# Up projection of a feed-forward layer as seven block products in place of eight, with weight sums made by accumulating DMA

## What is computed

```python
h = rmsnorm(x, norm_ffn_pre)
u = h @ w_up                              # (512, 1024) @ (1024, 5632): 2816 gate, 2816 value columns
u = conv_b + sum(conv_w[j] * shift(u, 2 - j) for j in range(3))   # causal, along the tokens
f = gelu(u[:, :2816]) * u[:, 2816:]
x = x + rmsnorm(f @ w_down, norm_ffn_post)
```

## Time and profile before

| | us |
|---|---|
| median of 3 runs | 632.87 (632.45 to 634.44) |
| profiled execution: device time | 632.87 |
| its span, first to last instruction | 631.1 |
| up projection, sweep 0 (in half units) | about 277 to 302 |
| up projection, sweeps 1 to 10 | 302 to 520 |
| down projection | 520 to 625 |

### The profile page before, as it was taken

The page is one execution under the profiler, slowest core; times in us unless marked ns, Lnnn a source line. Parts: engine busy times, 40 slices in busy tenths (PEclk is TensorE's granted clock), DMA queues, the critical chain, the costliest instruction groups (busy, mean ns, idle before and its releaser), DMA issues.

```text
span 631.1 us, 8616 instructions
## 1 busy us (share of the span) xinstructions
PE 618.7 (98%) x3048; PEld 510.3 (81%) x3048; DVE 418.0 (66%) x619; ACT 313.6 (50%) x505; POOL 102.1 (16%) x112
## 2 busy tenths in 40 slices
PE   7999999999999999999999999999999999999996
PEld 6888778778787877899888888888888888887885
DVE  3457548657755875984755556556565668988786
ACT  5457338526735834663533334343333336656661
POOL 5413103111210402421000000000000013532203
PEclk9999999999999999999999999999999999999999
DMA  9744223331513254642423233333323436999933
GB/s 273 205 124 136 76 68 100 101 95 41 159 38 98 103 206 160 196 138 69 133 86 104 79 98 100 100 100 93 107 84 103 162 69 112 180 226 230 230 88 133
DMA packets 91947, 78.90 MB, mean 125 GB/s; under 512 B 2617, under 2 KB 76521, under 8 KB 91922
## 3 DMA queue, kind: packets, MB, share of 16 engines
q1 hardware_dynamic: 84434, 61.79, 32.0%
q0 software_dynamic: 7488, 16.80, 13.3%
HBM read 76.46 MB, written 2.12 MB: 125 GB/s over the span
## 4 chain that ended last, share of the span: by engine, by line
PE 81%; DVE 7%; DMA 4%; POOL 3%; ACT 2%; issue 2%; DVEq 0%; SPq 0%; POOLq 0%; ACTq 0%
PE bank L539 73%; DVE ws L1490 2%; DMA raw<-in_w_down_dram 2%; PE bank L681 1%; PE bank L619 1%; DMA raw<-in_w_in_dram 1%; POOL grstd L473 1%; DMA late<-in_w_down_dram 1%; PE bank L670 1%; DVE xs L1306 1%; PE bank L610 1%; PE bank L609 1%; DVE hT L1466 1%; PE bank L550 1%; POOL work L477 1%
## 5 line engine op out<-in xcount | busy, mean ns | idle before, releaser
L539 PE MATMUL bank<-hT,ws 128*128 128x512 f32 (+1 forms) x1872 | 410.2, 375 | 1.6 <-DVE work L1284 0.6
L539 PEld LDWEIGHTS bank<-hT,ws 128*128 128x128 f32 x1872 | 328.7, 188 | 63.2 <-issue 2.5
L539 PE MATMUL bank<-ws,yT 128*128 128x512 f32 x468 | 110.0, 391 | 0.2 <-DVE late L1510 0.2
L1189 DVE TENSOR_TENSOR ws<-raw,ws 128x1024 fp32r<-128x1024 f32 x85 | 103.5, 1218 | 6.9 <-ACT ws L875 6.4
L539 PEld LDWEIGHTS bank<-ws,yT 128*128 128x128 f32 x468 | 87.0, 188 | 18.5 <-DVE late L1510 0.6
L875 ACT ACTIVATE ws<-raw 128x1024 fp32r<-128x1024 f32 x88 | 92.6, 1053 | 15.5 <-PE bank L539 11.5
L1096 ACT ACTIVATE gains<-bank,conv 128x512 f32<-128x512 f32 x22 | 17.2, 781 | 76.8 <-PE bank L539 76.8
L1450 DVE SCALAR_TENSOR_TENSOR gains<-bank,conv,gains 128x511 f32<-128x511 f32 x22 | 16.5, 749 | 53.8 <-ACT gains L1096 53.8
L522 POOL DMA_DIRECT2D late<-in_w_down_dram x8 | 10.7, 1335 | 253.2 <-DVE ws L1490 253.2
L1096 ACT ACTIVATE rot<-bank,conv 128x512 f32<-128x512 f32 x22 | 17.2, 780 | 63.8 <-PE bank L539 63.8
L539 PE MATMUL bank<-ws,hT 128*128 128x512 f32 x186 | 42.8, 389 | 0.0
(11 more groups left out here) (135 smaller groups left out, 605.9 us busy)
## 6 DMA issues: line engine op xcount, KB each, us to landing
raw<-in_w_up_dram SPq DMA_DIRECT2D x44, 512.0 KB, 3.8
raw<-in_w_in_dram SPq DMA_DIRECT2D x28, 512.0 KB, 4.3
raw<-in_w_out_dram SPq DMA_DIRECT2D x16, 512.0 KB, 3.3
raw<-in_w_down_dram POOLq DMA_DIRECT2D x12, 512.0 KB, 7.7
raw<-in_w_down_dram SPq DMA_DIRECT2D x9, 512.0 KB, 4.2
late<-in_w_down_dram POOLq DMA_DIRECT2D x8, 512.0 KB, 5.8
xs<-in_x_dram SPq DMA_DIRECT2D x6, 512.0 KB, 4.1
late<-in_w_down_dram SPq DMA_DIRECT2D x6, 512.0 KB, 7.3
```

The lines of the kernel that those rows point to most:

```text
L539: return nc.tensor.matmul(dst, st, mv, start=start, stop=stop, skip_group_check=onto)
L1189: nc.vector.tensor_tensor(ws[:, c, 1, :], raw[:, c, :], f32(ws[:, c, 0, :]), ALU.subtract).then_inc(w_lo, 1)
```

## The change

Sweeps 0 and 1 stay as they are (`PLAIN = 2`); sweep 1 uses the other four banks. From sweep 2 on, a sweep is a 2x2x2 block product. The blocks of its output are gate and value columns (256 each) by left and right half of the tokens (256 each); the contraction is halved (4 tiles of 128 rows). Seven products take the place of eight: each is one unit of 2 column tiles x 4 row tiles x 3 matmuls = 24 matmuls, of 256 columns. Four sums of h blocks (`tF`) are made by DVE and split once, at the start; hF keeps a copy of h for this (`h_keep`). The weight sums are accumulating DMAs from POOL (`up_add`). The products run in the order 7, 1, 4, 3 of the sweep before, 6, 2, 5. Their results are joined in part in PSUM (products 6, 5, 3 and 4 accumulate onto what is there, "onto") and in part by ACT copies (`kept7`, `s1`, `kept4`) and DVE sums (`vneg` left and right, `c11`). The value half comes out negated, and its taps are stored negated. The taps, gelu and product of a sweep run beside the next sweep. Weight splits run three units ahead in place of two. `F_EARLY`, the f differences and the start of the down projection are reordered. The diff, cut:

```diff
+PLAIN = 2
+UP_UNITS = [("plain", i, j) for i in range(PLAIN) for j in range(4)]
+for _i in range(PLAIN, SWEEP - 1):
+    UP_UNITS += [(7, _i), (1, _i), (4, _i)] + [(3, _i - 1)] * (_i > PLAIN) + [(6, _i), (2, _i), (5, _i)]
+UP_UNITS += [(7, SWEEP - 1), (1, SWEEP - 1), (4, SWEEP - 1), (6, SWEEP - 1), (3, SWEEP - 2), (5, SWEEP - 1),
+             (2, SWEEP - 1), (3, SWEEP - 1)]
+UP_LOADS = {7: (0, 0), 1: (0, 0), 4: (1, 1), 2: (0, 1)}
+UP_ADDS = {7: (1, 0), 6: (1, 1), 3: (0, 1), 5: (1, 0)}
+DOWN0 = UP0 + len(UP_UNITS)
...
-F_EARLY = {(2, 1): (0,), (4, 1): (1,), (6, 1): (2,), (6, 3): (3,), (8, 1): (4,), (8, 3): (5,), (9, 1): (6,), (10, 1): (7,)}
-F_SLOTS = 16
-F_AHEAD = 6
+F_EARLY = {(4, 7): (0,), (4, 8): (1,), (4, 9): (2,), (4, 10): (3,), (6, 10): (4,), (5, 10): (5,), (2, 10): (6,)}
+F_DIFF = {(4, 3): 0, (4, 5): 1, (1, 8): 2, (1, 10): 3}
+F_SLOTS = 17
+F_AHEAD = 5
...
+    return {7: i % 2, 6: i % 2, 3: i % 2, 4: 2 + i % 2, 5: 2 + i % 2, 1: 4, 2: 5}[p]
...
+        hF = part(5120, 2048).rearrange("p (k c) -> p k c", k=KT)
+        tF = [part(7168 + 1024 * m, 1024).rearrange("p (k c) -> p k c", k=4) for m in range(4)]
+        T_OF = {7: 0, 4: 1, 6: 2, 5: 3}
...
+        UP_BANK = [(0, 1, 5, 6), (2, 3, 4, 7)]
+        X_BANK, Y_BANK = [(0, 1), (2, 3)], [(5, 6), (4, 7)]
...
+            for i in range(PLAIN, SWEEP):
+                for p in (4, 1, 7, 2):
+                    n = UP0 + UP_AT[p, i]
+                    if raw_slot_of(n) < 4 or i > PLAIN:
+                        sp.wait_ge(w_lo, lo_count(before_in_slot(n)))
+                    sp.dma_start(up_raw(n).rearrange("p (k n) -> p k n", k=4), up_block(UP_LOADS[p], i)
...
+            def up_add(p, i):
+                n = UP0 + UP_AT[p, i]
+                c = raw_slot_of(n)
+                if p == 7:
+                    pool.wait_ge(raw_loaded[c], 16 * loads_of_slot(n))
+                else:
+                    pool.wait_ge(w_lo, lo_count(before_in_slot(n)))
+                pool.dma_start(up_raw(n).rearrange("p (k n) -> p k n", k=4), up_block(UP_ADDS[p], i),
+                               accum_op=ALU.add).then_inc(raw_added[c], 16)
+            up_add(7, PLAIN)
+            for i in range(PLAIN, SWEEP):
+                up_add(6, i)
+                up_add(5, i)
+                if i + 1 < SWEEP:
+                    up_add(7, i + 1)
+                up_add(3, i)
...
+            def up_product(n):
+                p, i = UP_UNITS[n]
+                c, done = slot_of(UP0 + n), i - PLAIN
+                pe.wait_ge(w_lo, lo_count(UP0 + n))
+                if p in T_OF:
+                    pe.wait_ge(t_lo, T_OF[p] + 1)
+                if p == 7:
+                    if done < 2:
+                        pe.wait_ge(gtap0, 2 * (i - 1))
+                        pe.wait_ge(vtap0, 2 * (i - 1))
+                    else:
+                        pe.wait_ge(c11_done, done - 1)
+                if p == 1:
+                    pe.wait_ge(gtap0, 2 * (i - 1))
+                    if done < 2:
+                        pe.wait_ge(vtap0, 2 * (i - 1))
+                if p == 4:
+                    pe.wait_ge(p7_kept, done + 1)
+                if p == 6:
+                    pe.wait_ge(p1_kept, done + 1)
+                if p == 2:
+                    pe.wait_ge(p4_kept, done + 1)
+                if p == 5:
+                    pe.wait_ge(v_left, done + 1)
+                if p == 3:
+                    pe.wait_ge(v_right, done + 1)
+                onto = p in (6, 5, 3, 4)
+                lo = 0 if p in (7, 4) else 256
+                for r in range(2):
+                    b = (X_BANK if p in (1, 6, 5, 3) else Y_BANK)[i % 2][r]
+                    for k in range(4):
+                        cols = slice(k * 256 + r * P, k * 256 + r * P + P)
+                        for m in range(3):
+                            ins = three(bank[b][:, lo:lo + 256], ws[:, c, 0, cols], ws[:, c, 1, cols],
+                                        t_block(p, 0)[:, k, :], t_block(p, 1)[:, k, :], m,
+                                        not onto and k == 0 and m == 0, k == 3 and m == 2, onto)
+                ins.then_inc(unit_done, 1)
...
+            def up_post(n):
+                act.wait_ge(unit_done, UP0 + n + 1)
+                if n < 4 * PLAIN:
+                    _, i, j = UP_UNITS[n]
+                    if j % 2 == 0:
+                        gate_tap2(i, j // 2, bank[UP_BANK[i][j]][:])
+                    else:
+                        value_tap2(i, j // 2, bank[UP_BANK[i][j]][:])
+                        gate_gelu(i, j // 2)
+                    return
+                p, i = UP_UNITS[n]
+                done = i - PLAIN
+                x, y = X_BANK[i % 2], Y_BANK[i % 2]
+                if p == 7:
+                    if done:
+                        act.wait_ge(v_right, done)
+                    for r in sides(y):
+                        ins = nc.scalar.activation(kept7[:, r, :], both(y[r], 0, 256), ACT.Copy)
+                    ins.then_inc(p7_kept, 1)
+                if p == 1:
+                    if done >= 2:
+                        act.wait_ge(c11_done, done - 1)
+                    nc.scalar.activation(s1[:, done % 2], both(x, 256, 512), ACT.Copy).then_inc(p1_kept, 1)
+                if p == 4:
+                    if done:
+                        act.wait_ge(v_left, done)
+                    for r in sides(y):
+                        ins = nc.scalar.activation(kept4[:, r, :], both(y[r], 0, 256), ACT.Copy)
+                    ins.then_inc(p4_kept, 1)
+                if p == 3 and i < SWEEP - 1:
+                    act.wait_ge(c11_done, done + 1)
+                    for r in range(2):
+                        gate_tap2(i, r, bank[x[r]][:])
+                if i < SWEEP - 1:
+                    if p == 6 and done:
+                        gate_gelu(i - 1, 0)
+                    if p == 2 and done:
+                        gate_gelu(i - 1, 1)
+                    if p == 5:
+                        act.wait_ge(v_right, done + 1)
+                        for r in range(2):
+                            value_tap2(i, r, vneg[:, r, :])
+                elif p == 2:
+                    gate_gelu(i - 1, 0)
...
+            AHEAD = 3
+            up_split_hi(4)
+            for m in range(2):
+                blocks_hi(m)
+            for n in range(len(UP_UNITS)):
+                if n + AHEAD < len(UP_UNITS):
+                    if n + AHEAD > 4:
+                        up_split_hi(n + AHEAD)
+                else:
+                    down_hi(n + AHEAD - len(UP_UNITS))
+                up_post(n)
+                if n == 1:
+                    blocks_hi(2)
+                if n == 3:
+                    blocks_hi(3)
+                for m in F_EARLY.get(UP_UNITS[n], ()):
+                    f_hi_of(m)
+            gate_gelu(SWEEP - 2, 1)
+            for r in range(2):
+                value_tap2(SWEEP - 1, r, vneg[:, r, :])
+            act.wait_ge(c11_done, SWEEP - PLAIN)
+            for r in range(2):
+                gate_tap2(SWEEP - 1, r, bank[X_BANK[(SWEEP - 1) % 2][r]][:])
+            f_hi_of(AHEAD + F_AHEAD - 1)
+            down_hi(AHEAD)
+            f_hi_of(AHEAD + F_AHEAD)
+            for r in range(2):
+                gate_gelu(SWEEP - 1, r)
             last = {p: DOWN_AT[p, COUPLES - 1] for p in range(1, 8)}
...
+            def c11(i):
+                dve.wait_ge(p1_kept, i - PLAIN + 1)
+                x, y = X_BANK[i % 2], Y_BANK[i % 2]
+                for r in sides(y):
+                    ins = nc.vector.tensor_tensor(both(x[r], 0, 256), both(y[r], 256, 512), s1[:, (i - PLAIN) % 2, r, :], ALU.add)
+                ins.then_inc(c11_done, 1)
+            def up_post(n):
+                if n < 4 * PLAIN:
+                    _, i, j = UP_UNITS[n]
+                    src = bank[UP_BANK[i][j]][:]
+                    if j % 2 == 0:
+                        gate_taps(i, j // 2, src)
+                    else:
+                        value_taps(i, j // 2, src)
+                        f_tile(i, j // 2)
+                    return
+                p, i = UP_UNITS[n]
+                done = i - PLAIN
+                x = X_BANK[i % 2]
+                dve.wait_ge(unit_done, UP0 + n + 1)
+                if p == 7 and done:
+                    value_taps(i - 1, 0, vneg[:, 0, :])
+                if p == 1 and done:
+                    value_taps(i - 1, 1, vneg[:, 1, :])
+                if p == 3:
+                    if i == SWEEP - 1:
+                        f_tiles(i - 1)
+                    c11(i)
+                if p == 6:
+                    dve.wait_ge(p4_kept, done + 1)
+                    if done:
+                        dve.wait_ge(vtap0, 2 * i)
+                    nc.vector.tensor_tensor(vneg[:, :, 0:256], both(x, 256, 512), kept4, ALU.add).then_inc(v_left, 1)
+                if p == 5:
+                    dve.wait_ge(p7_kept, done + 1)
```

(43 more changed lines are left out.)

280 lines of the change are left out of this document (184 added, 96 removed).

## The result

The changed kernel takes 694.77 us (693.79 to 697.55, 4 runs) against 633.62 us before: a ratio of 1.098 (95% interval 1.095 to 1.100), 61 us slower. The profiled execution has a span of 692.0 us against 631.1, 60.9 more. The forecast was 682 with a range of 662 to 706.

A forecast was written before the change was run, and what follows sets the result against it. PE bound the old kernel; in the new one DVE and ACT's lock step would set 27.9 us loops. Loop stalls 49 plus tail 9, less 13 saved, plus clock 4 gave 682 us; own range 664 to 693, wider 662 to 706.

The forecast's parts named there:

- What PE saves: Up-stage sweeps: 168 matmuls at 0.121 us, 20.3 us against 21.76, saving 13.1 us over nine sweeps.
- DVE and ACT in lock step: Up-stage loop from c11 to c11: fixed DVE and ACT orders make it 26.1 us before any DMA.
- the four handovers: Four places per loop where DVE idles for ACT's half of a split: 2.5, 1.65, 1.65 and 2.5, together 8.3 us.
- The other signs: Up stage: PE idle before products 4 and 5, about 5 and 2.5 us, and DVE busy near 65%.
- Late sums: Accumulating DMA for product 7's weights lands 1.8 us late in each loop, making the loop 27.9 us.
- the rival of a price by number: Accumulating DMA packets cost 176 ns each whatever their bytes: loop about 31 us, time 703 to 725; chance 10%.
- The clock: PE's granted clock falls in some of the loops' stalls: +4 us, bounds 0 and +15.
- falls in every long stall: Rival: PE's clock falls seven to eight times at 2 us each, time 693 to 698; chance 15%.
- The start: Entry to the loops: PE enters ahead and the first loop hides about 4 us of 53 idle, leaving 49.
- The end: Tail between the last product and the fifth down unit: 9 us, bounds 5 to 13.
- Floor and end: PE's saving of 13 us over the sweeps taken with the 9 us tail before the down stage: -4.
- The rival that PE sets the time: Up-stage loops: DVE and ACT keep up, loop under 20.3 us, time 620; chance 6%.

The follow-up runs named there:

- e4: The changed kernel with both e1's reordered ACT list and e2's tiny weight sums: 626.83 us.
- e7: The changed kernel with e2's tiny weight sums and e3's 30 idle matmuls before product 4: 674.48 us.
- e2: The changed kernel with the up stage's accumulating DMAs adding 16 columns of one row tile in place of 512 KB: 677.49 us.
- e8: The changed kernel with a third buffer for the weights of products 7, 6 and 3, ACT's list unchanged: 686.06 us.
- e1: The changed kernel with ACT's steps that wait for DVE (tap2, gelu) moved behind the next unit's split: 662.77 us.
- e12: e5 with SP loading sweep 2's product 7 first and the three buffers taken in another turn: 626.42 us, 0.989 of the kernel before.
- e3: The changed kernel with 30 idle PE matmuls of 256 columns in the stall before product 4 of sweeps 3 to 10: 696.09 us.
- e5: e1 plus a third buffer for the weights of products 7, 6 and 3, against the changed kernel: 635.11 us.

## Why the prediction was right, and by how much its terms were off

The direction, the size (+49 forecast, +61 measured) and the mechanism held. The measured sum, in the same parts: the floor (e4) is 623.8 us of span, 7.3 under the kernel before; the first c11 of the change is 8.6 us behind e4's (361.1 and 352.5); its eight loops take 59.5 us more than e4's; behind the last c11 both take 115. -7.3 + 8.6 + 59.5 = 60.8. The 59.5 are 44.1 for the order of the lists (e7 less e4), 7.1 for the clock (e2 less e7) and 8.3 for late sums (the change less e2; e8 gives 9.5). These shares hold for this order of taking things away. With the lists put right first, the lists, with what part of the clock's price goes with them, are 35.4 (the change less e1), and the late sums 24.1 (e1 less e4): while the lists hold the loops, they hide most of what the sums cost.

- *What PE saves.* 168 matmuls at 0.121 was right to 1% (20.16 us, 0.120 each). The spacing of the earlier trace rows for halves in sweep 0 carried over to another stage. The floor is 7.3 us under the kernel before: the 13 us forecast, less what the seam to the down projection costs (below).

  The Trainium skill, "TensorE: Matmul & The Clock Gate", section "Wait — 56ns, not 53.3ns?", by its columns at 2.4 GHz plus about 2.5 ns, would have had 18.3 us a loop as an estimate; e4 and e12 at 20.16 us disagree with it.
- *DVE and ACT in lock step.* Forecast 26.1 us a loop; e7 has 25.6 to 26.9 in the first six, 29.8 in the seventh and 14.0 in the short last one. The first six average 26.1. Right, and the four handovers are as worked out: 2.51, 1.71, 1.71 and 2.62 us in e7, together 8.6 where 8.3 was forecast. The other signs that it named are there too: PE idle 4.6 to 4.7 us before product 4 and 0.3 to 2.4 before product 5, DVE busy for 64% from 324.2 to 573.6 us.
- *Late sums.* Forecast 1.8 us in each of seven loops, 12.6; measured 8.3 to 9.5 in all, 1.2 to 1.4 a loop. It isn't a steady lateness, as forecast: ACT's waits for product 7's sum are 1.7, 1.2, 2.6, 0, 0.3, 0.8 and 2.4 us. A landing of 6.7 us was taken and the median is 6.5, which explains only 0.2; why the lateness differs from loop to loop stays open. Packets cost nearly by bytes: those of the sums take 106 ns each at 1 KB, against 176 at 2 KB, so the rival of a price by number is out. No row of before could exclude it. The queues of the changed kernel, 325 to 540 us (packets, MB, share of 16 engines), from which 0.524 x 16 x 215 us / 16934 is 106 ns, and the median landing of the sums, 6.5 us:

```profile
q0 software_dynamic: 16934, 16.82, 52.4%
q1 hardware_dynamic: 16368, 16.25, 24.7%
...
raw<-in_w_up_dram POOLq DMA_DIRECT2D x33, 512.0 KB, 6.5
```

- *The clock.* Forecast +4 with bounds 0 and 15; measured 7, and in the change it fell after all of the long stalls, not some: product 4's unit took 4.4 to 5.3 us in every loop. The case "falls in every long stall" was the right one in what the clock does, but its price of 2 us each was double the measured 0.9, since PE isn't what the loop waits for in all of that time. The times that the rival gave, 693 to 698, don't follow from its own price either: 678, the forecast without the clock, plus seven to eight times 2 is 692 to 694. That the measured 694.8 lies among them is chance: 7 us of it are the clock, and the start, which the rival doesn't have, makes up most of the rest.
- *The start.* This step failed: the forecast gave 4 us back for PE's lead in the first loop. Even with tiny sums nothing was hidden: e2's first loop is 26.8 us, the next 27.1. In its place the first sum is late: the load of product 7 stands third in SP's list, behind that of product 4 and the wait for its buffer, and the sum goes behind the load (e12). That is 8.6 us on the other side (8.3 if counted from the start of the 192 matmuls), 12.6 from the forecast's term, and the main reason why the time is 12.8 us over the forecast. The chain for 7 was worked out for a running loop alone; the same chain at the start, 11.5 us of waiting in the list and a landing beside three other loads, was not.
- *The end.* 9 us forecast, with bounds 5 and 13; PE's stalls there are 2.1 us before the first down unit and 4.2 before the fifth, 6.4 in all. e12 still has 4.7 before the fifth. Floor and end together, -7.3 where -4 was forecast.
- *The rival that PE sets the time* was wrong for this kernel and right for the one with ACT's list reordered and its sums in time: from 380 to 500 us of e12 DVE is busy for 105.6 of 120 us, 88% as forecast, and PE for all 120. The forecast gave 620 for it; it is 626, with the seam's stall.

Against the forecast's terms: lists 44.1 where 7 x 5.8 = 40.6 was forecast, sums 8.3 where 12.6, clock 7.1 where 4, floor and end -7.3 where -4, start +8.6 where -4. The differences are +3.5, -4.3, +3.1, -3.3 and +12.6, together 11.6: all but the start nearly cancel. That the other four cancel is luck: had they all pointed up, they would have added 14 us to the start's 12.6. The time lies just outside its own range of 664 to 693, inside the wider one only by the room left for the rivals.

## What to carry to other kernels

Two engines with hand-written orders need a third number beside their busy shares: each place where A's next instruction stands on B's list behind something that waits for what A has just done costs the whole of B's step, and this adds up around the loop whatever the bound engine does. To find it, follow one period of both lists with a finger, from a row of before; to mend it, put on B's list what A needs next ahead of what waits for A. When a limit is taken away, measure what stands behind it before judging the idea: here the order cost 44 us, and the clock 7, buffers and start-up some 17 behind it, and only with all of them gone did the seven products win 1.1%. What a second limit costs is seen only once the first is gone: late sums were 8 us beside the bad order and 24 without it. And a queue of loads is such a list too: the first load waited 11.5 us for a buffer that another one needed.

## What the runs showed of the hardware

The granted clock of the changed kernel fell to 1.2 GHz after each of PE's stalls of 4.6 to 4.7 us in the loops and not after those of 0.3 to 2.4, and product 4 then took 4.4 to 5.3 us in place of 2.9. The length of the stall alone doesn't tell: before product 5 the clock fell after stalls of 2.1 us in e3 and of 2.8, 3.3 and 4.0 in e1 (48 matmuls then took 7.3 us in place of 5.8, the clock 0.76 to 0.77 on average), and not after stalls of 2.3 in e3 and of 2.95 in e1. With the 16 DMA engines at a share of 1.00 (e5) the loops were exactly as long as at 0.36 (e4, both 380 to 500 us), so even a full set of engines cost nothing once each transfer was asked for early enough. Moving an early load from third to first place in SP's list, into a buffer that was free sooner (e12), took 8.1 us off the stretch from the 192 matmuls to the first c11 of e5 (10.6 off the first c11 itself, since e5's profiled execution came 2.5 us later to that stretch) and 8.7 us off its time.
